# Expert stage of a mixture-of-experts trunk: three column chunks of 512, 512 and 384 in place of four of 352, down blocks two to a unit, weight rings of six 8 KB places in place of nine of 5.5 KB

## What is computed

```python
def swiglu(x, w_gu, w_dn):
    g, u = jnp.split(x @ w_gu, 2, axis=-1)
    return (jax.nn.silu(g) * u) @ w_dn

for ex in range(N_EXPERTS):                       # 8, D_MODEL 1024, D_EXPERT 1408
    y = y + gates[:, ex:ex + 1] * swiglu(xf, w_gu[ex], w_dn[ex])
```

## Time and profile before

| | us |
|---|---|
| median of 3 runs (2938.02 to 2946.98) | 2938.19 |
| profiled execution | 2944.82 |
| its span, first to last instruction | 2943.0 |
| first `m_hi` to the last start of a split of `m_lo` | 2072.1 to 2891.8 |
| busy in the span: PE / DVE / ACT | 2658.4 / 1677.2 / 1475.3 |

### The profile page before, as it was taken

The page is one execution under the profiler, slowest core; times in us unless marked ns, Lnnn a source line. Parts: engine busy times, 40 slices in busy tenths (PEclk is TensorE's granted clock), DMA queues, the critical chain, the costliest instruction groups (busy, mean ns, idle before and its releaser), DMA issues. The chain is left out here.

```text
span 2943.0 us, 46503 instructions
## 1 busy us (share of the span) xinstructions
PE 2658.4 (90%) x16139; PEld 2316.4 (79%) x16139; DVE 1677.2 (57%) x2404; ACT 1475.3 (50%) x2301; POOL 390.7 (13%) x521
## 2 busy tenths in 40 slices
PE   3897979999999899998989988888899999999993
PEld 1786967787886588887867768877799999999993
DVE  2145655545555633232241138864788898988886
ACT  1223755555543233332132236651788887878783
POOL 2033211011101220000030024404200000000002
PEclk6997979989999999999999989998899999999997
DMA  8431000000002512222234510031999999999995
GB/s 308 154 122 25 1 6 1 1 1 1 1 2 115 200 48 72 78 71 79 79 107 149 197 69 17 15 110 46 347 386 382 386 380 386 380 382 378 383 378 207
DMA packets 263957, 474.66 MB, mean 161 GB/s; under 512 B 29536, under 2 KB 202720, under 8 KB 257680
## 3 DMA queue, kind: packets, MB, share of 16 engines
q1 hardware_dynamic: 256208, 448.20, 43.2%
q0 software_dynamic: 4416, 14.70, 1.3%
q10 hardware_dynamic: 3200, 9.97, 0.9%
HBM read 456.30 MB, written 16.49 MB: 161 GB/s over the span
## 5 line engine op out<-in xcount | busy, mean ns | idle before, releaser
L3102 DVE TENSOR_TENSOR m_lo<-m_raw,m_hi 128x1408 fp32r<-128x1408 f32 (+1 forms) x459 | 649.3, 1457 | 66.4 <-ACT m_hi L2961 65.7
L2961 ACT ACTIVATE m_hi<-m_raw 128x1408 fp32r<-128x1408 f32 (+1 forms) x459 | 550.8, 1246 | 50.4 <-DMA m_raw<-moe_w_gu 35.6
L213 PE MATMUL acc<-w_hi,h_hi 128*128 128x512 f32 (+1 forms) x1120 | 430.5, 384 | 27.2 <-DVE w_lo L195 13.5
L195 DVE TENSOR_TENSOR w_lo<-w_raw,w_hi 128x1024 fp32r<-128x1024 f32 (+1 forms) x132 | 161.0, 1223 | 491.5 <-ACT w_hi L190 490.7
L215 PE MATMUL acc<-w_hi,h_lo 128*128 128x512 f32 (+1 forms) x1120 | 424.4, 379 | 0.0
L214 PE MATMUL acc<-w_lo,h_hi 128*128 128x512 f32 (+1 forms) x1120 | 424.3, 379 | 0.0
L190 ACT ACTIVATE w_hi<-w_raw 128x1024 fp32r<-128x1024 f32 (+1 forms) x134 | 135.1, 1014 | 468.6 <-PE acc L215 409.0
L213 PEld LDWEIGHTS acc<-w_hi,h_hi 128*128 128x128 f32 x1120 | 212.7, 190 | 81.4 <-issue 23.7
L215 PEld LDWEIGHTS acc<-w_hi,h_lo 128*128 128x128 f32 x1120 | 212.7, 190 | 34.2
L214 PEld LDWEIGHTS acc<-w_lo,h_hi 128*128 128x128 f32 x1120 | 213.0, 190 | 32.5
L2879 PE MATMUL p_gates<-m_hi,x_hi 128*128 128x352 f32 x544 | 181.5, 334 | 5.0 <-DVE m_lo L3102 5.0
(11 more groups left out here) (389 smaller groups left out, 5364.1 us busy)
## 6 DMA issues: line engine op xcount, KB each, us to landing
m_raw<-moe_w_gu SPq DMA_DIRECT2D x544, 352.0 KB
m_raw<-moe_w_dn SPq DMA_DIRECT2D x187, 512.0 KB
ada_w<-ada_w SPq DMA_DIRECT2D x48, 1024.0 KB, 5.9
w_raw<-ffn_w_gu SPq DMA_DIRECT2D x88, 256.0 KB, 2.9
w_raw<-w_in_o SPq DMA_DIRECT2D x24, 512.0 KB, 5.8
w_raw<-ffn_w_dn SPq DMA_DIRECT2D x22, 512.0 KB, 3.6
w_raw<-w_in_e SPq DMA_DIRECT2D x28, 384.0 KB, 3.4
scratch_y_slots<-y_slot ACTq DMA_DIRECT2D x18, 512.0 KB, 6.3
```

Source lines behind the costliest of these rows:

```text
L195: eng.tensor_tensor(lo, self.raw_of(c, k), hi, ALU.subtract).then_inc(self.lo.sem, 1)
L213: eng.matmul(out, hi, whi[:, b, :], start=first, stop=False)
L2961: a.activation(whi[:, u % MSPLIT, 0:size(u)], raw[:, s, 0:size(u)], ACT.Copy).then_inc(s_hi.sem, 1)
L3102: dve.tensor_tensor(wlo[:, u % MSPLIT, 0:n], raw[:, u % MRAW, 0:n], whi[:, u % MSPLIT, 0:n], ALU.subtract).then_inc(s_lo.sem, 1)
```

## The change

- The chunks are columns 0 to 511, 512 to 1023 and 1024 to 1407. A gate and up unit has 2048 floats in a partition in the first two chunks (8 units) and 1536 in the third (4 units).
- A down unit has two blocks (2048 floats, one transfer), the last one a single block. A slot tile has 12 + 6 = 18 units in place of 16 + 11 = 27.
- Both rings have 6 places of 2048 floats, in place of 9 of 1408.
- Matmuls into `p_gates` and `p_ups` are 512, 512 and 384 columns wide: 96 and 48 in place of 192 of 352. Those of the downs stay 66 of 512.
- There are 3 activation transposes of 4, 4 and 3 blocks in place of 4 of 2, 3, 3 and 3. PE runs them after u = 5, 9 and 13, and `turn_x` after u = 15. ACT and DVE run SiLU and product after u = 6, 10 and 14, `part_a` after u = 7, 11 and 15, `part_x` after u = 17, which is the last unit, and the copy of `p_down` after u = 3.
- POOL gathers the next tokens once all turns of a slot tile are done, as before.

```diff
-MRAW, MSPLIT = 9, 9
-MUNIT = 2 * 2 * 352
-ECH = 352
+MRAW, MSPLIT = 6, 6
+ECH = 512
+MUNIT = 2 * 2 * ECH
...
-    CH, KU = D_EXPERT // ECH, J // 2
+    CHUNKS = [(c, min(c + ECH, D_EXPERT)) for c in range(0, D_EXPERT, ECH)]
+    CH, KU = len(CHUNKS), J // 2
     GU, DN = CH * KU, D_EXPERT // P
-    NU = GU + DN
+    NU = GU + (DN + 1) // 2
...
-    TA = ((0, 2), (2, 5), (5, 8), (8, 11))
-    X_USES, A_USES = (3, 4), (0, 1, 2, 5)
-    AT_Y, AT_SILU, AT_PART_A, AT_PART_X = 4, (8, 12, 16, 20), (11, 15, 19, 23), 21
+    TA = [(c // P, n // P) for c, n in CHUNKS]
+    X_USES, A_USES, BANKS = (3, 4), (0, 1, 2), (0, 1, 0, 1, 0)
+    AT_Y, AT_SILU, AT_TURN_A, AT_PART_A, AT_TURN_X, AT_PART_X = 3, (6, 10, 14), (5, 9, 13), (7, 11, 15), 15, 17
...
-                        src = wdn[bass.ds(e, 1), :, u - GU, :].rearrange("e p n -> p (e n)")
-                        sp.dma_start(raw[:, s, 0:D], src).then_inc(landed[s].sem, 32)
+                        ks_of = blocks(u)
+                        src = wdn[bass.ds(e, 1), :, ks_of[0]:ks_of[-1] + 1, :].rearrange("e p j n -> p (e j) n")
+                        sp.dma_start(down(raw, u), src).then_inc(landed[s].sem, 32)
...
-                    if u in (7, 11, 15):
-                        turn_a(tile, (u - 7) // 4)
-                    if u == 16:
+                    if u in AT_TURN_A:
+                        turn_a(tile, AT_TURN_A.index(u))
+                    if u == AT_TURN_X:
                         pe.wait_ge(s_gather.sem, s_gather.at(tile * 16 + 32))
                         for half in range(2):
-                            turn_x(use(tile, X_USES[half]), half)
-                    if u == 19:
-                        turn_a(tile, 3)
+                            turn_x(use(tile, X_USES[half]), half, BANKS[X_USES[half]])
```

More of the change, by code:

```diff
@@ L2733, in tail_stage @@
         idx = K.sb(ctx, "slot_tokens", [P, SLOT_TILES + 1], I32)
-        K.sb(ctx, "gap", [P, 1000])
+        K.sb(ctx, "gap", [P, 2000])
         tok, idx0 = K.sb(ctx, "token_ids", [P, NT], I32), K.sb(ctx, "first_tokens", [P, 1], I32)
@@ L2746, in tail_stage, with width, blocks, size @@
         wdn = I["moe_w_dn"][0].rearrange("e (j p) n -> e p j n", p=P)
+        def width(c):
+            return CHUNKS[c][1] - CHUNKS[c][0]
+        def blocks(u):
+            return range(2 * (u - GU), min(2 * (u - GU) + 2, DN))
+        def size(u):
+            return 4 * width(u // KU) if u < GU else len(blocks(u)) * D
         def gu(ring, u):
-            return ring[:, u % ring.shape[1], :].rearrange("p (j h n) -> p j h n", j=2, h=2)
-        def size(u):
-            return MUNIT if u < GU else D
+            return ring[:, u % ring.shape[1], 0:size(u)].rearrange("p (j h n) -> p j h n", j=2, h=2)
+        def down(ring, u):
+            return ring[:, u % ring.shape[1], 0:size(u)].rearrange("p (k n) -> p k n", n=D)
     def use(tile, j):
@@ L2842, in _, with turn_x @@
             mm.then_inc(s_first.sem, 1)
-            def turn_x(n, half, first=False):
-                if not first:
+            def turn_x(n, half, bank):
+                if n is not None:
                     pe.wait_ge(s_tlo.sem, s_tlo.at(n - 1))
                 for j in range(4):
-                    mm = pe.transpose(pT[:, half ^ (0 if first else 1), j * P:(j + 1) * P], xg[:, 4 * half + j:D:J], K.ident[:])
+                    mm = pe.transpose(pT[:, bank, j * P:(j + 1) * P], xg[:, 4 * half + j:D:J], K.ident[:])
                 mm.then_inc(s_turned.sem, 1)
@@ L2854, in turn_a @@
                 pe.wait_ge(s_act.sem, s_act.at(tile * CH + (c + 1)))
-                pe.wait_ge(s_tlo.sem, s_tlo.at(use(tile, A_USES[c]) - 1))
+                pe.wait_ge(s_tlo.sem, s_tlo.at(use(tile, A_USES[c]) - (0 if c == 0 else 1)))
                 for j in range(a, b):
-                    mm = pe.transpose(pT[:, A_USES[c] % 2, (j - a) * P:(j - a + 1) * P], act[:, j * P:(j + 1) * P], K.ident[:])
+                    mm = pe.transpose(pT[:, BANKS[A_USES[c]], (j - a) * P:(j - a + 1) * P], act[:, j * P:(j + 1) * P], K.ident[:])
                 mm.then_inc(s_turned.sem, 1)
@@ L2861, in _ @@
             for half in range(2):
-                turn_x(half, half, first=True)
+                turn_x(None, half, half)
             with pe.Fori(0, SLOT_TILES) as tile:
@@ L2870, in _ @@
                         if k == 0:
-                            pe.wait_ge(s_act.sem, s_act.at(tile * CH + (c - 1)))
+                            pe.wait_ge(s_act.sem, s_act.at(tile * CH + (c - 1 if c else 0)))
                         pe.wait_ge(s_lo.sem, s_lo.at(tile * NU + (u + 1)))
@@ L2878, in _ @@
                             for half, acc in ((0, pG), (1, pU)):
-                                pe.matmul(acc[:, c % 2, 0:ECH], xh[:, j, :], h[:, b, half, :], start=start, stop=False)
-                                pe.matmul(acc[:, c % 2, 0:ECH], xh[:, j, :], l[:, b, half, :], start=False, stop=False)
+                                pe.matmul(acc[:, c % 2, 0:width(c)], xh[:, j, :], h[:, b, half, :], start=start, stop=False)
+                                pe.matmul(acc[:, c % 2, 0:width(c)], xh[:, j, :], l[:, b, half, :], start=False, stop=False)
@@ L2881, in _ @@
                             for half, acc in ((0, pG), (1, pU)):
-                                mm = pe.matmul(acc[:, c % 2, 0:ECH], xl[:, j, :], h[:, b, half, :], start=False, stop=stop)
+                                mm = pe.matmul(acc[:, c % 2, 0:width(c)], xl[:, j, :], h[:, b, half, :], start=False, stop=stop)
                         mm.then_inc(s_used.sem, 1)
                     else:
-                        k = u - GU
-                        if k == 0:
+                        if u == GU:
@@ L2888, in _ @@
                             pe.wait_ge(s_y.sem, s_y.at(tile + 1))
[L2889 to L2896, removed]
@@ L2897, in _ @@
-                        for half in range(2):
-                            cs = slice(half * 512, half * 512 + 512)
-                            mm = pe.matmul(pD[:, half, :], al[:, k, :], whi[:, s, cs], start=False, stop=k == DN - 1)
+                        for i, k in enumerate(blocks(u)):
+                            for c in range(CH):
+                                if k == TA[c][0]:
+                                    pe.wait_ge(s_tlo.sem, s_tlo.at(use(tile, A_USES[c]) + 1))
+                            if i == 0:
+                                pe.wait_ge(s_lo.sem, s_lo.at(tile * NU + (u + 1)))
+                            h, l = down(whi, u), down(wlo, u)
+                            for half in range(2):
+                                cs = slice(half * 512, half * 512 + 512)
+                                pe.matmul(pD[:, half, :], ah[:, k, :], h[:, i, cs], start=k == 0, stop=False)
+                                pe.matmul(pD[:, half, :], ah[:, k, :], l[:, i, cs], start=False, stop=False)
+                            for half in range(2):
+                                cs = slice(half * 512, half * 512 + 512)
+                                mm = pe.matmul(pD[:, half, :], al[:, k, :], h[:, i, cs], start=False, stop=k == DN - 1)
@@ L2949, in part_a @@
                 a.wait_ge(s_turned.sem, s_turned.at(use(tile, A_USES[c]) + 1))
-                a.activation(ah[:, x:y, :], pT[:, A_USES[c] % 2, 0:(y - x) * P].rearrange("p (j n) -> p j n", n=P), ACT.Copy).then_inc(s_thi.sem, 1)
+                a.activation(ah[:, x:y, :], pT[:, BANKS[A_USES[c]], 0:(y - x) * P].rearrange("p (j n) -> p j n", n=P), ACT.Copy).then_inc(s_thi.sem, 1)
             for half in range(2):
@@ L2970, in _ @@
                         c = AT_SILU.index(u)
-                        a.wait_ge(s_used.sem, s_used.at(tile * NU + 4 * (c + 1)))
+                        a.wait_ge(s_used.sem, s_used.at(tile * NU + KU * (c + 1)))
                         a.wait_ge(s_act.sem, s_act.at(tile * CH + c))
-                        a.activation(silu[:], pG[:, c % 2, 0:ECH], ACT.Silu).then_inc(s_silu.sem, 1)
+                        a.activation(silu[:, 0:width(c)], pG[:, c % 2, 0:width(c)], ACT.Silu).then_inc(s_silu.sem, 1)
                     if u in AT_PART_A:
@@ L2978, in _ @@
                         for half in range(2):
-                            part_x(use(tile, X_USES[half]), half, half ^ 1)
+                            part_x(use(tile, X_USES[half]), half, BANKS[X_USES[half]])
             n = SLOT_TILES
@@ L3090, in part_a @@
                 dve.wait_ge(s_thi.sem, s_thi.at(use(tile, A_USES[c]) + 1))
[L3091 removed]
+                dve.tensor_tensor(al[:, x:y, :], pT[:, BANKS[A_USES[c]], 0:(y - x) * P].rearrange("p (j n) -> p j n", n=P),
                                   ah[:, x:y, :], ALU.subtract).then_inc(s_tlo.sem, 1)
@@ L3130, in _ @@
             for tile in range(1, SLOT_TILES + 1):
-                pool.wait_ge(s_turned.sem, s_turned.at(2 if tile == 1 else NTURN * (tile - 2) + 7))
+                pool.wait_ge(s_turned.sem, s_turned.at(2 if tile == 1 else NTURN * (tile - 2) + 2 + NTURN))
```

5 lines of the change are left out of this document (3 added, 2 removed).

## The result

The changed kernel takes 2990.87 us (median of 4 runs, 2986.27 to 2997.16), the kernel before in the same comparison 2938.11 (2930.11 to 2946.98): a ratio of 1.0166, with a 95% interval of 1.0145 to 1.0188. It is slower by 53 us; the forecast was 2972.7 in a range of 2953 to 2996. The profiled execution has a span of 2984.9 us.

A forecast was written before the change was run, and what follows sets the result against it. PE was taken to bound the kernel. Wider matmuls -15.3, boundary waits +36.5, waits ahead of the downs +12.1 and first unit +1.2 gave +34.5 us on 2938.2, so 2972.7 us, range 2953 to 2996.

The forecast's parts named there:

- The bound: In the expert loop before, PE sets the pace: 48.24 us a slot tile, with transfers next at 47.9.
- -0.90 us for the wider matmuls: Gate and up matmuls fall from 31.10 to 30.20 us a slot tile, -15.3 us over 17.
- Transfers at nothing: Weight transfers with longer rows and six-place rings cost nothing: 45.4 to 47.9 us, under the slot tile's length.
- The end of a slot tile: Token transposes, split, table load and unit 0's split take 7.29 us; PE stands 2.28 at 16 boundaries, +36.5.
- The drain: About 1380 ns at a table switch would make the boundary wait 3.66 us, total 2995; not counted, chance 0.05.
- Ahead of the downs: Chunk 1's transposes to the first down unit's split take 5.34 us; PE stands 0.71, 17 times, +12.1.
- The clock: Rival: PE's gaps drop its clock at boundaries, losing 1.9 us at each of 16, 3003 us; chance 0.07.
- a granted clock under 1.00 in mid loop: Sign in the profile after that would make the forecast wrong: PE's clock below its full level within the loop.
- the first unit: At the loop's start, the first wider unit arrives 1.2 us later, once.
- both waits at their high bounds: Boundary wait 2.9 us and wait before the downs 1.1 give +51.0 us, 2989.
- The rivals of the other sign: Faster, both waits hidden, 2924 us, chance 0.05; or unchanged, one wait hidden or transfers holding PE, 2932, chance 0.05.
- no change: Rival: one wait hidden, or transfers hold PE at 47.9 us a slot tile, 2932 us; chance 0.05.

The follow-up runs named there:

- e3: Changed kernel with tokens transposed after unit 12 and split after 14, and chunk 1's activations split after unit 12: 2923.95 us, ratio 0.9938.
- e1: Changed kernel with the next tokens transposed after unit 12 in place of 15 and split after unit 14 in place of 17: 2940.04 us, ratio 1.000.
- e8: Changed kernel with eight unread matmuls of 512 columns added on PE after each slot tile's last unit: 2979.25 us, ratio 1.0139.
- e2: Changed kernel with only the split of chunk 1's activations moved, after unit 12 in place of 11: 2988.40 us, ratio 1.0170.
- e6: Changed kernel with the tokens split after unit 16 in place of 17, PE's transposes still after 15: 3009.72 us, ratio 1.0221.

## Why the prediction was right, and where its sizes were off

- **The bound.** PE set the pace in the kernel before, which the prediction read from the list of waits and not from the shares. e3 bears it out: with both waits gone the slot tile takes 47.35 us, where the forecast had 47.34 for PE's own work. The term of -0.90 us for the wider matmuls is right to 0.01.
- **Transfers at nothing.** Right: in no run's loop does PE wait for a landing, and e3's slot tile of 47.35 lies under the 47.9 that was the transfers' time with short rows, at 391 GB/s.
- **The end of a slot tile.** The chain was forecast at 7.29 us and took 7.34. The wait was forecast at 2.28 and cost 2.46 (changed kernel against e1). What was missed is mostly PE's restart: its first unit after a stand takes 2.88 us in place of 2.72.
- **The drain.** By the Trainium skill's "ScalarE: Activation LUTs", section "What ACT_TABLE_LOAD costs", 1.38 us more would have stood in this chain. The trace disagrees in this place: 1.28 of load, 1.29 to the next instruction.
- **Ahead of the downs.** Chain 5.34 forecast, 5.42 measured; wait 0.71 forecast, 0.92 measured (e1 against e3), again with a slower restart: the first six matmuls behind the gap take 1.46 us in place of 1.36. The list of waits gives this gap as 0.65 and it costs 0.92, because it counts from the modelled end of the last matmul, 0.17 us behind the place where the next could have started, and leaves the restart out.
- **The clock.** This is the step that failed, as I put it: "a gap of 2.3 us in dense work need not cost the 2.4 GHz level", with 0.07 for a fall. It did cost it, at 5 of 16 boundaries in the profiled execution, and with that came one of the prediction's own signs of being wrong, "a granted clock under 1.00 in mid loop". The rows I read the earlier trace rows were single gaps. The first holds one of 3.44 us without a fall, which says little of 16 in a row. The second I misread: I had its 0.62 come "after longer sparse work". The stretch ahead of it has PE busy 4.43 of 5 us at clock 1.00; it ends in 16 matmuls of 8 columns, and behind them stands a gap of 2.88 us. The lines, for the first and then for the second:

```profile
1969.16 0.47 PE L213 MATMUL acc<-w_hi,h_hi 128*128 128x512 f32 x1 [3.44 <-issue]
```

```profile
2026.00:2031.00 5.00, 4.43 (x33) 4.02 (x31) 2.36 (x4) 0.01 (x1) 2.32 (x3) 1.00 0.25 99
```

```profile
2028.58 1.85 PE L2820 MATMUL p_route<-router_w,h_turned 128*128 128x8 f32 x16
2033.31 1.97 PE L2811 MATMUL norm_bank<-ident,norm_h 128*128 128x128 f32 x8 [2.88 <-POOL norm_h L475]
```

So the trace of before already held a fall around a gap not much longer than the one forecast, and 0.07 was too low. The price was near: 1.9 us forecast, 1.5 measured. The Trainium skill's "TensorE: Matmul & The Clock Gate", section "HAM oscillation — how this bites in real kernels", tells of longer waits than this one that do so at each pass; here gaps of 2.2 us were enough for some.
- **The sum with measured terms:** 17 x (47.35 - 48.24) = -15.1, 16 x 2.46 = +39.4, 17 x 0.92 = +15.6, and +1.2 for the first unit (PE's first wait is 6.2 us, and 5.04 in the earlier trace rows): +41.1, where the forecast had +34.5. The two waits were mis-sized by 6.5 together. The profile's five falls add 7.6: +48.7. Between the medians stand 52.8. The 11.6 between the changed kernel and e8 would fill the rest, but it is a difference between medians of four runs each from two comparisons, and the other runs have no profile to count falls in; some 4 us stay open. Inside the two profiles the account closes: from the loop's first matmul of `p_gates` to that of its last slot tile stand 774.0 us before and 820.2 after, 46.2 more, and 16 x (-0.89 + 2.46 + 0.92) with the four falls in this stretch is 45.8.
- **Where luck helped.** With both waits at their high bounds the forecast ended at 2989, and the measured 2990.87 lies above that. It is inside the range by the room left for the drain, which did not occur; what filled it was the clock, which the range was said to leave out.
- **The rivals of the other sign.** The waits were not hidden, and no run has the transfers as the bound. e1 shows how near "no change" was: with the boundary's wait gone, the saving of 0.89 us and the remaining wait of 0.92 cancel, and the ratio is 1.000.

Left open: which boundaries the clock falls at. e2, whose slot tiles are shorter, had 14 falls and the changed kernel 5, with the same gap of 2.17 us, and e6 had 11 with gaps of 2.64 us; no run varies the slot tile's length alone. A kernel without the table load ahead of unit 0 was not tried.

## What to carry to other kernels

When a step that waits for another engine is moved in an in-order list, ask what that engine has left to do from the event waited for to the place where it needs the waiter, and set against it everything that stands behind the wait, down to the first thing handed over: here 5.0 us of transposes and down blocks against 7.3 of token split, table load and unit split. Coarser units lengthen each such chain by a unit's growth on every engine it passes, even where their total work falls. Moving the wait nearer or farther in the waiter's own list helps only if work that the other engine needs gets ahead of it (e2), and hurts if work falls behind it (e6); what helped most was to have the event itself three units sooner, and the wait for it too (e1, e3; the event alone was not moved).

## What the runs showed of the hardware that I had not expected

- TensorE's granted clock falls from 2.4 to 1.2 GHz after gaps of 2.2 to 2.3 us in otherwise full work, at some boundaries and not at others (5 of 16, 4 of 16, 14 of 16), and at 11 of 16 after gaps of 2.64 us; with gaps of 0.97 us there was no fall in 16. One costs 1.5 to 1.6 us.
- Eight matmuls whose results nothing reads, put into a wait of 2.2 us by the list, took 24 us off the median of a kernel with 14 such falls in its profile, and 12 off one with 5 (20 and 9 between profiled executions).
- A saving can be paid back by the clock: e2 took 0.9 us out of each slot tile and gained 2.5 us where 14 were due.
- The first 12 matmuls of 512 columns behind a wait of 2.17 us took 2.88 us in place of 2.72, at full clock.
